# Output products of the gated blocks, column half by column half, with modulation loads placed anew: a two-block network in float32 on one core

## The reference

```python
def swiglu(h, w_in, w_out):
    g, u = jnp.split(h @ w_in, 2, axis=-1)
    return (jax.nn.silu(g) * u) @ w_out
x = layer_norm(ALPHA * x + g1 * y_lat, ln_g[i, 0], ln_b[i, 0])
x = layer_norm(ALPHA * x + g2 * swiglu(modulate(x, sh2, sc2), ffn_w_in[i], ffn_w_out[i]),
               ln_g[i, 1], ln_b[i, 1])
...
x = x + (jax.nn.silu(gate) * up) @ w_ffn_out[layer]
```

## Time and profile before

| | |
|---|---|
| time, median of 3 runs | 1127.8 us (1127.6 to 1129.52) |
| profiled execution | 1133.1 us, of which span 1131.3 us |
| TensorE busy | 1095.4 us, 97% of the span |
| VectorE busy | 829.3 us, 73% |
| ScalarE busy | 546.0 us, 48% |
| mean granted TensorE clock | 0.992 |
| moved by DMA | 236.91 MB, mean 209 GB/s |

### The profile page before, as it was taken

The page is one execution under the profiler, slowest core; times in us unless marked ns, Lnnn a source line. Parts: engine busy times, 40 slices in busy tenths (PEclk is TensorE's granted clock), DMA queues, the critical chain, the costliest instruction groups (busy, mean ns, idle before and its releaser), DMA issues.

```text
span 1131.3 us, 15971 instructions
## 1 busy us (share of the span) xinstructions
PE 1095.4 (97%) x6209; PEld 907.2 (80%) x6209; DVE 829.3 (73%) x1292; ACT 546.0 (48%) x842; POOL 101.0 (9%) x86
## 2 busy tenths in 40 slices
PE   4999999999999989999999999999999999999998
PEld 2876777888888767888888898878777788888887
DVE  2588788699999788988674686778664877676753
ACT  1436236364454332554553466757565436454542
POOL 0000000000000002000000002055556000000000
PEclk9999999999999999999999999999999999999999
DMA  9998773767988777466955556433342545666552
GB/s 339 336 323 202 273 261 109 279 208 249 336 289 317 293 268 255 143 223 186 300 197 198 159 172 209 163 112 115 125 135 95 166 146 153 186 187 186 186 191 107
DMA packets 145020, 236.91 MB, mean 209 GB/s; under 512 B 4901, under 2 KB 86322, under 8 KB 144690
## 3 DMA queue, kind: packets, MB, share of 16 engines
q1 hardware_dynamic: 138128, 221.12, 58.2%
q10 hardware_dynamic: 6818, 14.78, 4.3%
HBM read 229.33 MB, written 6.55 MB: 209 GB/s over the span
## 4 chain that ended last, share of the span: by engine, by line
PE 54%; DVE 4%; ACT 1%; issue 1%; POOL 1%; POOLq 0%; DVEq 0%; ACTq 0%
PE bank L698 52%; PE bank L835 2%; DVE ring_lo L1959 1%; POOL ring_lo L2925 1%; DVE aux L2822 0%; ACT h L1537 0%; DVE y_tok L2825 0%; DVE y_tok L2293 0%; DVE small L2295 0%; DVE y_tok L2289 0%; ACT w_hi L1528 0%; PE bank L894 0%; DVE aux L2784 0%; DVE small L2766 0%; ACT y_tok L1931 0%
## 5 line engine op out<-in xcount | busy, mean ns | idle before, releaser
L1959 DVE TENSOR_TENSOR ring_lo<-ring,w_hi 128x1024 fp32r<-128x1024 f32 (+4 forms) x290 | 337.3, 1198 | 145.9 <-ACT w_hi L1528 145.7
L1528 ACT ACTIVATE w_hi<-ring 128x1024 fp32r<-128x1024 f32 (+3 forms) x312 | 313.9, 1039 | 252.4 <-PE bank L698 207.7
L698 PE MATMUL bank<-h,w_hi 128*128 128x512 f32 (+1 forms) x1152 | 362.9, 379 | 0.2
L698 PE MATMUL bank<-h,ring_lo 128*128 128x256 f32 x1056 | 281.3, 280 | 0.0
L698 PEld LDWEIGHTS bank<-h,w_hi 128*128 128x128 f32 x1152 | 203.6, 188 | 45.7 <-issue 2.8
L698 PE MATMUL bank<-w_hi,h 128*128 128x512 f32 (+4 forms) x640 | 192.9, 385 | 2.9 <-ACT big L1814 1.8
L698 PEld LDWEIGHTS bank<-h,ring_lo 128*128 128x128 f32 x1056 | 193.1, 189 | 0.5 <-issue 0.5
L698 PEld LDWEIGHTS bank<-w_hi,h 128*128 128x128 f32 x640 | 119.7, 190 | 26.3 <-issue 4.2
L698 PE MATMUL bank<-ring_lo,h 128*128 128x512 f32 (+4 forms) x320 | 115.6, 380 | 0.0
L698 PE MATMUL bank<-w_hi,ff_hi 128*128 128x512 f32 x264 | 103.8, 393 | 4.2 <-ACT w_hi L1528 3.7
L698 PE MATMUL bank<-ring_lo,ff_hi 128*128 128x512 f32 x264 | 103.3, 391 | 0.0
(11 more groups left out here) (274 smaller groups left out, 1338.7 us busy)
## 6 DMA issues: line engine op xcount, KB each, us to landing
aux<-in_w_mod SPq DMA_DIRECT2D x24, 2048.0 KB, 9.4
ring<-in_ffn_w_in SPq DMA_DIRECT2D x88, 512.0 KB, 5.3
ring<-in_w_in SPq DMA_DIRECT2D x24, 1024.0 KB, 4.9
ring<-in_ffn_w_out SPq DMA_DIRECT2D x22, 1024.0 KB, 5.3
ring<-in_w_ffn_in SPq DMA_DIRECT2D x44, 512.0 KB, 4.7
ring<-in_attn_w_qkv SPq DMA_DIRECT2D x12, 1024.0 KB, 13.0
ring<-in_w_ffn_out SPq DMA_DIRECT2D x11, 1024.0 KB, 5.1
bias_rows<-srow ACTq DMA_DIRECT2D x1, 5376.0 KB
```

The lines of the kernel that those rows point to most:

```text
L698: return nc.tensor.matmul(o, l, r, start=start, stop=stop, **kw)
L1528: nc.scalar.activation(half_of(i, 0, half), raw_half(i, half), ACT.Copy).then_inc(w_hi, 1)
L1959: V.tensor_tensor(half_of(i, 1, half), raw_half(i, half), half_of(i, 0, half).bitcast(F32), ALU.subtract).then_inc(w_lo, 1)
```

## The change

The output stage of each gated block goes over all 22 chunks for the left columns first, then over all 22 for the right. Group 0 is now two panels of 2 x 512, one at the head of each half, so the stage has 12 panels in place of 11 (`ffn0`: 38 to 43 left, 44 to 49 right). VectorE does the left residual pieces in the middle of the right half, behind the low parts of the panels right 1 and right 2 (45 and 46 in `ffn0`). Before the right pieces it now also does the low part of the panel behind the stage. In `ffn0`, `mod_sums(8)` moves behind left 5 and `mod_sums(10)` behind right 5, and the loads of modulation halves 17, 18 and 19 move to later panels.

```diff
--- before.py
+++ after.py
@@ -156,12 +156,9 @@
-        for kg, (lo, hi) in enumerate(OUT_GROUPS):
-            if hi - lo <= PK // 2:
-                add((name + "_out", 0, kg), w_out, kg, hi - lo, 0, 2 * NB, lo)
-            else:
-                for nb in range(2):
-                    add((name + "_out", nb, kg), w_out, kg, hi - lo, nb * NB, nb * NB + NB, lo)
+        for nb in range(2):
+            for kg, (lo, hi) in enumerate(OUT_GROUPS):
+                add((name + "_out", nb, kg), w_out, kg, hi - lo, nb * NB, nb * NB + NB, lo)
@@ -820,6 +817,32 @@
+            def gemm_by_columns(stage, lhs, inputs, sums, pool):
+
+                last = OUT_GROUPS[-1][1] - 1
+                for nb in range(2):
+                    for kg, (lo, hi) in enumerate(OUT_GROUPS):
+                        key, final = (stage, nb, kg), hi - 1 == last
+                        w = panel(key, True, final)
+                        if kg == 0:
+                            for tt in range(TT):
+                                take((stage, nb, tt), pool)
+                        for half, cs_ in ((None, range(lo, hi)),) if final else by_half(key, lo, hi):
+                            for tt in range(TT):
+                                for c in cs_:
+                                    if nb == 0 and tt == 0:
+                                        for k in inputs(c):
+                                            wait_emptied(pe, k)
+                                    ins = product(psum[where[(stage, nb, tt)][0]], lhs(tt, c),
+                                                  [x[:, c - lo, :] for x in w], c == 0, c == last)
+                                if final:
+                                    fills(ins, (stage, nb, tt))
+                            if half == 0:
+                                release_first_half(key, ins)
+                        release(key, ins, (stage, nb, TT - 1) if final else None)
+                        if (nb, kg) in sums:
+                            mod_sums(sums[nb, kg])
@@ -973,9 +996,8 @@
-                gemm_by_tile(name + "_out", lambda tt, c: token_tile(ffT, c, tt), OUT_GROUPS,
-                             lambda c: (ff_key(name, c // 2),), {2: 8, 5: 10} if name == "ffn0" else {},
-                             pool=PAIR_POOL[name])
+                gemm_by_columns(name + "_out", lambda tt, c: token_tile(ffT, c, tt), lambda c: (ff_key(name, c // 2),),
+                                {(0, 5): 8, (1, 5): 10} if name == "ffn0" else {}, PAIR_POOL[name])
@@ -2304,11 +2326,22 @@
+            def residual_first_half(stage, gate):
+
+                i = panel_at[(stage, 1, 1)]
+                split_to(i)
+                residual_piece(stage, gate, 0, 0)
+                split_to(i + 1)
+                residual_piece(stage, gate, 0, 1)
+
             def residual_stats(stage, gate, used, last):
 
                 split_to(last)
-                residual_piece(stage, gate, 0, 0)
-                residual_piece(stage, gate, 0, 1)
+                if stage in ("wo", "poolw"):
+                    residual_piece(stage, gate, 0, 0)
+                    residual_piece(stage, gate, 0, 1)
+                else:
+                    split_to(last + 1)
                 residual_piece(stage, gate, 1, 0)
@@ -2448,11 +2481,11 @@
             mod_product(16, [1])
-            split_to(first + 7)
+            residual_first_half("ffn0_out", g2row)
             mod_product(16, [2, 3])
-            split_to(first + 8)
+            split_to(first + 9)
             mod_product(17, [0, 1])
-            split_to(first + 9)
+            split_to(first + 10)
             mod_product(17, [2, 3])
@@ -2468,6 +2501,7 @@
+            residual_first_half("ffn1_out", g2row)
             residual_stats("ffn1_out", g2row, g2_used, last_panel("ffn1_out", 1))
@@ -2906,8 +2940,11 @@
+            split_to(panel_at[("ffn2_out", 1, 1)])
+            for tt in range(TT):
+                residual("ffn2_out", 0, tt)
             split_to(last_panel("ffn2_out", 1))
-            for nb in range(2):
+            for nb in range(1, 2):
                 for tt in range(TT):
                     residual("ffn2_out", nb, tt)
@@ -2991,7 +3028,7 @@
             halves_before = {RING: [0], 5: [1], 6: [2], 8: [3], 10: [4, 5], 11: [6], 12: [7], 15: [8], 17: [9], 25: [10],
-                             28: [11], 31: [12], 33: [13], 36: [14], 39: [15], 42: [16], 43: [17], 48: [18], 50: [19]}
+                             28: [11], 31: [12], 33: [13], 36: [14], 39: [15], 42: [16], 48: [17], 55: [18], 58: [19]}
```

## The result

| | before | after |
|---|---|---|
| median | 1128.87 us (1127.6 to 1130.33, 5 runs) | 1132.09 us (1131.77 to 1134.24, 5 runs) |
| profiled execution | 1133.1 us, span 1131.3 | 1132.05 us, span 1130.0 |
| ratio | | 1.0035, 95% interval [1.0024, 1.0047] |

The change makes the kernel slower by 0.35%, about 3.9 us (2.7 to 5.3); the medians differ by 3.2 us. The two profiled executions don't show that: after's is the shorter, because the one of before (1133.1 us) is longer than each of the five runs in the table.

The account below looks back on a forecast made before the run. TensorE, busy 97% of the span, was taken as the bound. New waits of 9.0 us less 5.8 us gone, with the last piece 0.65 us closer, gave +2.6 us: 1127.8 + 2.6 = 1130.4 us, range 1125.6 to 1133.0.

Parts of the forecast that it names:

- Step 1: First block, panel left 1: TensorE waits 1.1 us for VectorE's first low half.
- Step 2: First block, panel left 2: TensorE waits 0.6 us, VectorE starting it behind earlier vector work and a modulation product.
- Step 3: First block, left 4, its DMA behind half 16: wait 2.8 us with a 12.1 us landing, 1.3 at 10.6.
- Step 4: First block, left 5: wait 0.4 us for VectorE; its DMA no longer waits for modulation.
- Step 5: First block, right 0: wait 2.0 us, its low part queued behind the eviction of modulation 8's sums and a product.
- Step 6: First block, right 1: wait 1.6 us, VectorE having other work ahead of its low part.
- slower still: First block: left 4's wait brings the lower clock back, +4.2 us, 1132.0 us; chance 0.15.
- Step 7: First block, right 3: about 0.5 us late behind left pieces, low parts and modulation products.
- Gone: First block: old waits of 0.5 and 3.66 us and 1.6 us of low clock vanish, 5.8 us.
- faster: First block, left 5 and right 0: load order decides, VectorE keeps up; up to 6.4 us won, 1121.4; chance 0.13.
- Shorter ends: Block ends shorten since half the residual is done early: two blocks x 4.2 us, 1119.4; chance 0.02.
- Even exchange: First block: left 4 lands early, no step beyond 5 and 6 shows; +1.0 us, 1128.8; chance 0.25.

Follow-up runs that it names:

- e3: The changed kernel with the sums of modulation 8 ahead of left 5 instead of behind it; ratio to before 0.9996.
- e6: e4 with the load of modulation half 16 also moved, behind the panel it stood ahead of; ratio to before 0.9964.
- e9: The kernel before with group 0 of each gated block's output stage loaded by two DMAs in place of one; ratio to before 1.0002.
- e1: The kernel before with only the second and third gated blocks' output stages by columns; ratio to before 1.0003.
- e8: The kernel before with the ring's four buffers taken in the order 2, 3, 0, 1; ratio to before 0.9989.
- e2: The kernel before with only the first gated block's output stage by columns, and the change's modulation loads; ratio to before 1.0021.
- e5: e3 with the load of modulation half 16 behind left 4 in the queue, not ahead of it; ratio to before 0.9987.
- e7: The changed kernel with halves 17, 18 and 19 loaded at the places of the kernel before; ratio to before 1.0138.
- e11: The changed kernel with only the loads of halves 18 and 19 back at the end of the stage; ratio to before 1.0068.
- e10: The changed kernel with right 0's low part ahead of the eviction of modulation 8's sums on VectorE; ratio to before 1.0030.
- e12: e5 with the second block's output stage by row groups again; ratio to before 0.9971, median 1126.19 us.
- e4: The kernel before, its column order kept, with only the loads of halves 17, 18 and 19 moved later; ratio to before 0.9976.

## Why the prediction was right

Forecast +2.6 us with the case "slower by over 0.2%" likeliest; measured +3.9 (2.7 to 5.3). Median 1132.09, within the range, towards its upper end. The mechanism in the first block is as forecast: the eviction of the sums stands ahead of the low part of right 0, and e3 takes both away. The size is right in part by luck, since two terms were too large and offset each other. From the stage's first product to the sums behind it are 61.7 us in e6, which has no wait. Against that the old order lost 6.3 us in before's profile, 6.0 in e9's, 2.8 in e1's and 2.6 in e8's; the sum took 5.8. The new order lost 6.6 us in after's and 10.2 in e2's; the sum took 9.0.

Of the signs, the waits of about 2 us at right 0 and of 1 to 3 us at left 4 came, and the other two stages kept their 60 us. The stage of 71 us did not come in after's profile (68.3, against 68.0 before), only in e2's (71.9), and the wait one panel behind right 0 not in after's. By steps:

- **Step 1** (left 1, 1.1 us): no row in after's and e5's profiles, 0.2 in e2's, 0.4 and 0.5 in e3's and e7's, 0.7 in e11's, 1.2 and 1.3 in e10's and e12's. In the last two the stage had begun 0.6 to 0.9 us sooner after the first row of the block's length than in after's, which takes up most of it. On average half of what I took.
- **Step 2** (left 2, 0.6): 0.3 to 0.4 in each profile by columns.
- **Step 3** (left 4, 2.8, or 1.3 with the early landing): I took the landing of 12.1 us. It was 10.7 in after's profile, wait 1.22, and 12.4 in e2's, wait 2.90. Waits of 1.0 to 1.2 us stand in five of the six profiles with this order and load (after, e3, e7, e10, e11; e2 is the sixth). Both bounds were real, but the early one is the usual, though left 5 followed at once as I had argued for the late one; this term should have been 1.3. e5 shows the cause: with half 16 behind left 4 the wait is gone.
- **Step 4** (left 5, 0.4): no wait is recorded there where half 17 has moved.
- **Step 5** (right 0, 2.0): 2.14, 2.13, 2.13 and 2.14 us in after, e2, e11 and e7, at the place named. e3 shows that it is program order: the sums one panel earlier take it away. The Trainium skill ("TensorE: Matmul & The Clock Gate", Why this matters for your kernels) warns of idle gaps over some 3 us; by this alone a wait of 2.14 us would bring no lower clock. In the rows of after it did, and in e11's behind 2.13 us; in e2's and e7's it did not.
- **Step 6** (right 1, 1.6): 1.20 us in e2 and 1.23 in e7, where right 0 ran at full clock. In after and e11 right 0 was at the lower clock, and the 1.6 us that this costs took the place of the wait. The sum had left the clock out and this wait in; the case "slower still" had added the clock on top, behind step 3. In fact only one of the two is paid behind right 0, because VectorE's chain sets when right 1 can start: from the start of right 0 to that of right 1 are 4.4 us in after and 4.2 in e2. So the low clock itself cost some 0.2 us here. e10 has no low clock in this stage and the same time.
- **Step 7** (right 3, 0.5): 0.2 in e3, e5, e7 and e12, no row in after.
- **Gone** (5.8 us): with step 3 the term that was mis-sized. It was taken from one profile in which the panel behind half 17 landed late (12.1 us: wait 3.66 and low clock 1.6). Four profiles of the old order with the old loads have lengths of 202.65, 202.06, 200.09 and 199.87 us, two late and two early landings; with the early one 1.4 + 0.9 (e1) or 1.2 + 0.8 (e8) goes, no clock. The mean over the four is 201.2 us; that over after and e2, 205.1. That the difference, 3.9, is the measured one is chance: e2's profile is the slowest of its runs, and e2's runs give the first block +2.4. With e1's +0.3 and the 0.8 us of the landing behind `cmp`, which neither e1 nor e2 has, that makes 3.5, an estimate from runs whose intervals are over a microsecond wide on either side. How the 3.9 us divide is open.
- **Last piece** (0.65 nearer): 0.45.
- **Second and third block, 0; halves 18 and 19 moved, 0**: e1 bears out the first within its noise. The second is not tested alone in the new order; what e11 shows is that leaving them would have cost 3.7 us, since right 5 is then held behind half 18. I had not seen that.
- **Not forecast**: the landing behind `cmp`, 1.3 us for ScalarE and 0.82 us of that on TensorE. It stands in the profiles of after, e3 and e7 (6.2 to 6.3 us), less in e5 (5.6) and e10 (5.4), not in e11, all with two more panels ahead; and in none of the eight with fewer (4.9 to 5.0 where I read the landing, ScalarE's wait at most 4.0). By e8 the other buffers alone don't bring it, by e9 two more DMAs alone don't; e11 shows that two panels more don't bring it always. Its cause stays open.

The rival "slower still" put the lower clock behind step 3's wait; that is what e2's profile shows, and not what after's does. The rival "faster" asked for new waits under 3.5 us in sum; steps 5 and 6 or the clock alone took 3.3 to 3.7. "Shorter ends" is refuted by e1. "Even exchange" is close: it had the early landing, but the gain from the old wait as in before's profile. Two of the rival "faster"'s figures don't follow from the sum: with half of the 9.0 us left the time is 1127.8 - 6.4 + 4.5 = 1125.9, not 1124, and the gain falls under 0.2% once the new waits pass 4.1 us, not 3.5. The base moved too: the median of before is 1128.87 over five runs, where the forecast had 1127.8 over three.

## What to carry to other kernels

When the order of products changes, a reduction that another engine evicts moves with it; look at what that engine has queued behind the eviction, and put the sums a panel ahead of where its chain must be through. A 2 MB load in the same queue ahead of a panel costs that panel its slack: place it behind the panel that is wanted next (e6, four numbers of a table, is 0.36% faster than before; no kernel with the new order in the first block had a lower ratio, the best is e12's 0.9971). And take a term that hangs on one landing from several profiles: the same code differed by 2.8 us in the block in question.

## What the runs showed of the hardware

- A 1 MB panel issued right behind a 2 MB load lands 10.2 to 12.4 us after issue, and not always alike for the same code: behind half 17 of the old order 10.2 (e1), 10.4 (e8), 11.7 (e9) and 12.1 us (before); behind half 16 ahead of left 4, 10.5 to 10.7 us in five profiles and 12.4 in e2. The Trainium skill ("DMA: Bandwidth & Descriptors", Queues, rings and completion order) says that descriptors are consumed in ring order and that completion need not be; the first agrees, since 1 MB panels of the second block's output stage, with no such load ahead, land in 5.0 us before and 5.1 after (medians). What decides between the early and the late time, no run here tells.
- The length of a wait does not tell by itself whether the lower clock follows. Directly behind the sums, at right 0, it followed waits of 2.14 us (after) and 2.13 us (e11) and did not follow 2.13 us (e2) and 2.14 us (e7). At 762 it followed 1.80 us in before and not 1.79 us in after. It also followed 2.90 (e2), 3.3 (e9), 3.3 (e11), 3.4 (e7), 3.66 and 6.09 us (e7), and did not follow 2.40 (e10, behind twelve products), 1.6 (e4) or 1.38 us (e1).
